# Three stage boundaries of a fused two-block kernel: next weights fetched and split early, attention's first maxima in two banks, first output tile begun in the merge

## The reference

```python
h = rms_norm(x, norm_gain[l]) * (1 + scale[:, None]) + shift[:, None]
aq, ak, av, ag, bz, bg, nq, nk, nv, ng = jnp.split(h @ w_in[l], SPLIT_POINTS, axis=-1)
```

```python
merged = gate_fox * (y_fox @ w_o_fox[i]) + gate_rwkv * (y_rwkv @ w_o_rwkv[i])
x = x + merged @ w_out[i]
h2 = rmsnorm(x, g_ffn[i])
```

## Time and profile before

| what | value |
|---|---|
| time, median of 3 runs | 3684.66 us (3683.51 to 3690.55) |
| the profiled execution's own time | 3686.16 us |
| its span, first to last instruction | 3684.2 us |
| TensorE (PE) busy | 3479.1 us, 94% |
| VectorE (DVE) busy | 2001.4 us, 54% |
| GpSimd (POOL) busy | 1869.1 us, 51% |
| ScalarE (ACT) busy | 1226.0 us, 33% |
| mean granted TensorE clock | 0.975 |

### The profile page before, as it was taken

The page is one execution under the profiler, slowest core; times in us unless marked ns, Lnnn a source line. Parts: engine busy times, 40 slices in busy tenths (PEclk is TensorE's granted clock), DMA queues, the critical chain, the costliest instruction groups (busy, mean ns, idle before and its releaser), DMA issues. The chain is left out here.

```text
span 3684.2 us, 53898 instructions
## 1 busy us (share of the span) xinstructions
PE 3479.1 (94%) x22186; PEld 2661.5 (72%) x22186; DVE 2001.4 (54%) x2268; ACT 1226.0 (33%) x1751; POOL 1869.1 (51%) x1036
## 2 busy tenths in 40 slices
PE   5999899899899999899999999989999999999999
PEld 5888544568788644578887777876578788878877
DVE  4443567662454477553656734545552888883141
ACT  3225444441223344432223422335411444431020
POOL 1444466543354466533445643314544799964443
PEclk9999999999999899999999999989999999999999
DMA  5112200225111200122221220020043122234202
GB/s 187 39 35 75 57 1 1 79 85 213 58 35 66 54 1 1 50 104 70 98 74 49 81 89 24 4 109 1 11 144 137 58 86 82 79 113 164 88 26 74
DMA packets 102074, 257.94 MB, mean 70 GB/s; under 512 B 29248, under 2 KB 38336, under 8 KB 100944
## 3 DMA queue, kind: packets, MB, share of 16 engines
q1 hardware_dynamic: 90960, 217.39, 17.3%
q10 hardware_dynamic: 10880, 37.23, 2.9%
HBM read 200.02 MB, written 54.56 MB: 69 GB/s over the span
## 5 line engine op out<-in xcount | busy, mean ns | idle before, releaser
L2083 PE MATMUL acc<-h_hi,weights_hi 128*128 128x512 f32 (+1 forms) x928 | 347.4, 374 | 8.2 <-DVE h_lo L2252 5.8
L1173 DVE TENSOR_REDUCE part_max<-aux 128x1 f32<-128x428 f32 (+5 forms) x468 | 253.0, 582 | 161.3 <-PE aux L977 113.7
L2084 PE MATMUL acc<-h_lo,weights_hi 128*128 128x512 f32 (+1 forms) x928 | 339.0, 365 | 0.0
L2085 PE MATMUL acc<-h_hi,weights_lo 128*128 128x512 f32 (+1 forms) x928 | 338.7, 365 | 0.0
L2808 PE MATMUL acc<-h_hi,weights_hi 128*128 128x512 f32 x672 | 271.3, 404 | 0.0
L2266 DVE RECIPROCAL arena<-arena 128x512 f32<-128x512 f32 (+1 forms) x48 | 141.7, 2953 | 223.2 <-ACT arena L2229 223.2
L2810 PE MATMUL acc<-h_hi,weights_lo 128*128 128x512 f32 x672 | 262.9, 391 | 0.0
L2809 PE MATMUL acc<-h_lo,weights_hi 128*128 128x512 f32 x672 | 262.5, 391 | 0.0
L1147 ACT ACTIVATE probs<-acc 128x1024 f32<-128x1024 f32 (+1 forms) x168 | 168.5, 1003 | 262.0 <-PE acc L1016 261.5
L1029 PE MATMUL acc<-probs,v_tok 128*64 128x512 f32 (+3 forms) x864 | 221.6, 593 | 2.5 <-DVE inverse L1195 2.5
L2083 PEld LDWEIGHTS acc<-h_hi,weights_hi 128*128 128x128 f32 x928 | 175.7, 189 | 42.7 <-issue 10.6
(11 more groups left out here) (560 smaller groups left out, 8925.5 us busy)
## 6 DMA issues: line engine op xcount, KB each, us to landing
weights<-in_w_in SPq DMA_DIRECT2D x44, 512.0 KB, 3.4
arena<-in_w_mod SPq DMA_DIRECT2D x6, 2048.0 KB, 9.9
weights<-in_w_up SPq DMA_DIRECT2D x24, 512.0 KB, 4.3
weights<-in_w_out SPq DMA_DIRECT2D x22, 512.0 KB, 4.7
weight_sums<-feed_forward_spill SPq DMA_DIRECT2D x22, 512.0 KB, 4.6
xT<-in_w_up SPq DMA_DIRECT2D x20, 512.0 KB, 4.3
mixer_gates<-arena SPq DMA_DIRECT2D x32, 256.0 KB, 2.1
weights<-in_w_gates SPq DMA_DIRECT2D x16, 512.0 KB, 3.8
```

The lines of the kernel that those rows point to most:

```text
L1173: nc.vector.tensor_reduce(part_max[:, b % 2, j, hh, i:i + 1], max_tile(m)[:, hh, 0:cw], AX_X, ALU.max, negate=True).then_inc(max_done, 1)
L2083: nc.tensor.matmul(out, w_hi[:, b, k, :], hi[:, k, cols], start=(k == 0), stop=False)
L2084: nc.tensor.matmul(out, w_hi[:, b, k, :], lo[:, k, cols], start=False, stop=False)
L2085: return nc.tensor.matmul(out, w_lo[:, b, k, :], hi[:, k, cols], start=False, stop=(k == KD - 1))
```

## The change

It has three parts. (a) Layer 0's `gemm_residual` also fetches and parts the first two tiles of layer 1's `w_in`, and layer 1's `project` takes them from there; before the means TensorE runs `keep_busy` 10, after them 4. (b) `rwkv_finish` ends with `keep_busy` 24 on TensorE; in the forgetting attention all eight pieces ahead go by turns to the two places, with waits to fit, and the pauses are 2 products each. (c) `gemm_merge` multiplies k-tiles 0 to 6 of output tile 0 into `aux`, and `gemm_residual` only k-tile 7 of it.

```diff
@@ multiply
     for b in range(2 if not maker else 0):
...
+        if first_in is not None and b == 0:
+            for c0, cn in chunks:
+                out, cols, k = first_in[:, c0:c0 + cn], slice(c0, c0 + cn), nk - 1
+                nc.tensor.matmul(out, w.hi[:, 0, k, :], rhs[0][:, k, cols], start=False, stop=False)
+                nc.tensor.matmul(out, w.hi[:, 0, k, :], rhs[1][:, k, cols], start=False, stop=False)
+                mm = nc.tensor.matmul(out, w.lo[:, 0, k, :], rhs[0][:, k, cols], start=False, stop=True)
+            mm.then_inc(acc_ready, 1)
             continue
@@ gemm_residual, SP
+                    for b, tile in enumerate(next_first):
+                        sp.wait_ge(w.parted, n + 1 + b)
+                        sp.dma_start(w.raw[:, b], tile).then_inc(w.loaded[b], 16)
@@ gemm_residual, TensorE (mean_by_two is False throughout)
                 if squares and not late:
                     if not beside:
                         keep_busy(pg, pg.aux[:, 1], 10)
-                    pe.wait_ge(sq_added, n - 1)
+                    else:
+                        pe.wait_ge(acc_free, n + 1)
+                        keep_busy(pg, pg.acc[:, 0], 10)
+                        pe.wait_ge(beside.added, n - 2)
+                    pe.wait_ge(sq_added, n - 2 if mean_by_two else n - 1)
...
                     mm.then_inc(mean_ready, 1)
                     if beside:
+                        keep_busy(pg, pg.acc[:, 0], 4)
@@ gemm_residual, GpSimd
                 part_weights(nc, pool, w, acc_ready, n)
+                for b in range(len(next_first)):
+                    pool.wait_ge(w.loaded[b], 16 * (n // 2 + 1))
+                    pool.wait_ge(acc_ready, n + 1 + b)
+                    nc.gpsimd.tensor_tensor(w.hi[:, b], w.raw[:, b], w.ones, ALU.mult).then_inc(next_rounded, 1)
+                    pool.wait_ge(next_rounded, b + 1)
+                    nc.gpsimd.tensor_tensor(w.lo[:, b], w.raw[:, b], full(w.hi[:, b]), ALU.subtract).then_inc(next_parted, 1)
@@ gemm_residual, VectorE
+                        done = first_in if first_in is not None and t == 0 else pg.acc[:, t % 2]
@@ pair_attention
+        m_ahead = [j for kind, j, *_ in order[:n_ahead] if kind == "max"] if own_keys else []
-            return score_slots[1].rearrange(...) if pieces[m][0] == 0 and m % 2 else pg.aux
+            return score_slots[1].rearrange(...) if (pieces[m][0] == 0 or m in m_ahead) and m % 2 else pg.aux
-                        if b >= 1:
+                        if b >= 1 and not (m in m_ahead and m - 1 in m_ahead):
                             pe.wait_ge(max_done, 2 * m - 1 + hh)
                         elif m >= 2:
                             pe.wait_ge(max_done, 2 * m - 3 + hh)
+                    if e == 1 and own_keys:
+                        pe.wait_ge(max_done, 2 * len(m_ahead))
-                            keep_busy(pg, outs[1], first_idle if j == 0 else 2 if pieces[j][0] == 0 else 4)
+                            keep_busy(pg, outs[1], first_idle if j == 0 else 2)
@@ project (layer 1 now as layer 0: SP's two fetches and POOL's two partings are gone)
-    done_before = 2 if opened else 0
+    done_before = 2
-                if not opened:
-                    fetch(0)
-                    fetch(1)
-                    keep_busy(pg, pg.acc[:, 0], 12 if opened else 36)
+                    keep_busy(pg, pg.acc[:, 0], 12)
@@ first_block
+                if l:
+                    weights = ahead.raw, ahead.hi, ahead.lo
+                              next_first=() if last else [I["w_in"][l + 1, t] for t in range(2)])
@@ gemm_merge, TensorE
                 multiply(pg, pe, w, y, pg.acc, MAIN, nk, acc_ready, acc_free, 2 * KD, turns=2, begun=True)
+                pe.wait_ge(ahead.parted, 2)
+                for k in range(KD - 1):
+                    pe.wait_ge(merged_parted, k + 2)
+                    for c, (c0, cw) in enumerate(MAIN):
+                        cols = slice(c0, c0 + cw)
+                        nc.tensor.matmul(pg.aux[:, c], ahead.hi[:, 0, k, :], hi[:, k, cols], start=(k == 0), stop=False)
+                        nc.tensor.matmul(pg.aux[:, c], ahead.hi[:, 0, k, :], lo[:, k, cols], start=False, stop=False)
+                        nc.tensor.matmul(pg.aux[:, c], ahead.lo[:, 0, k, :], hi[:, k, cols], start=False, stop=False)
@@ forgetting_attention: first_idle 4 becomes 2
@@ rwkv_finish, TensorE
+                pe.wait_ge(scaled, R_TILES - 1)
+                keep_busy(pg, pg.acc[:, 0], 24)
@@ second_block: gemm_residual(..., first_in=flat(pg.aux[:]))
```

More of the change, by code:

```diff
@@ L325, in part_weights, with multiply @@
             nc.gpsimd.tensor_tensor(w.lo[:, b], w.raw[:, b], full(w.hi[:, b]), ALU.subtract).then_inc(w.parted, 1)
-def multiply(pg, pe, w, rhs, acc, chunks, nk, acc_ready, acc_free, n, turns=1, maker=None, beside=None, begun=False):
+def multiply(pg, pe, w, rhs, acc, chunks, nk, acc_ready, acc_free, n, turns=1, maker=None, beside=None, begun=False, first_in=None):
     nc = pg.nc
@@ L436, in _, with gemm_residual @@
                                              func or ACT.Copy).then_inc(acc_free, 1)
-def gemm_residual(pg, cn, w_of, n, rhs, x, parts, nk, store=None, squares=None, maker_in=None, beside_in=None, x_source=None, ahead=None, following=None, late=False):
+def gemm_residual(pg, cn, w_of, n, rhs, x, parts, nk, store=None, squares=None, maker_in=None, beside_in=None, x_source=None, ahead=None, following=None, late=False, next_first=(), first_in=None):
     nc = pg.nc
@@ L459, in gemm_residual @@
             total, ring = squares[0], squares[1:]
+        next_rounded, next_parted = pg.sem("next_rounded"), pg.sem("next_parted")
+        mean_by_two = False
         with nc.Block() as block:
@@ L486, in _ @@
             def _(pe):
-                multiply(pg, pe, w, rhs, pg.acc, chunks, nk, acc_ready, acc_free, n, maker=maker, beside=beside)
+                multiply(pg, pe, w, rhs, pg.acc, chunks, nk, acc_ready, acc_free, n, maker=maker, beside=beside, first_in=first_in)
                 if squares and not late:
@@ L490, in _ @@
                         keep_busy(pg, pg.aux[:, 1], 10)
-                    pe.wait_ge(sq_added, n - 1)
+                    else:
[3 more added lines that the diff above has]
+                    pe.wait_ge(sq_added, n - 2 if mean_by_two else n - 1)
+                    if mean_by_two:
+                        pe.wait_ge(sq_ready, n)
+                    for t in range(width // P):
+                        cols = slice(t * P, (t + 1) * P)
+                        mm = nc.tensor.matmul(pg.aux[:, 0, t:t + 1], total[:, cols], cn["mean"][:, 0:1], start=True, stop=not mean_by_two)
+                        if mean_by_two:
+                            mm = nc.tensor.matmul(pg.aux[:, 0, t:t + 1], ring[(n - 1) % 2][:, cols], cn["mean"][:, 0:1], start=False, stop=True)
+                    mm.then_inc(mean_ready, 1)
                     if beside:
-                        pe.wait_ge(beside.added, n - 2)
-                    for t in range(width // P):
-                        mm = nc.tensor.matmul(pg.aux[:, 0, t:t + 1], total[:, t * P:(t + 1) * P], cn["mean"][:, 0:1], start=True, stop=True)
-                    mm.then_inc(mean_ready, 1)
+                        keep_busy(pg, pg.acc[:, 0], 4)
             @block.gpsimd
@@ L530, in _ @@
                         tile = x[:, t, c0:c0 + cn]
-                        up = nc.vector.scalar_tensor_tensor(tile, pg.acc[:, t % 2, c0:c0 + cn], 1.0 if scale is None else scale(t), tile,
+                        done = first_in if first_in is not None and t == 0 else pg.acc[:, t % 2]
+                        up = nc.vector.scalar_tensor_tensor(tile, done[:, c0:c0 + cn], 1.0 if scale is None else scale(t), tile,
                                                             ALU.mult, ALU.add)
@@ L543, in _ @@
                 elif squares:
-                    add_squares(n - 1)
+                    if not mean_by_two:
+                        add_squares(n - 1)
                     if beside:
@@ L931, in pair_attention @@
         wide = blocks[0][4]
+        m_ahead = [j for kind, j, *_ in order[:n_ahead] if kind == "max"] if own_keys else []
         def max_tile(m):
-            return score_slots[1].rearrange("p (h n) -> p h n", h=2) if pieces[m][0] == 0 and m % 2 else pg.aux
+            return score_slots[1].rearrange("p (h n) -> p h n", h=2) if (pieces[m][0] == 0 or m in m_ahead) and m % 2 else pg.aux
         def score_tile(e):
@@ L2113, in _ @@
             def _(pool):
-                if opened:
-                    pool.sem_inc(parted, 2)
+                pool.sem_inc(parted, 2)
                 for kind, i in order:
@@ L2399, in first_block @@
                 gemm_residual(pg, cn, weight_tiles(I["w_out"][l]), KD, h, x, parts, KD, store=x_dram, squares=squares, maker_in=maker_in,
-                              beside_in=None if last else next_in, ahead=ahead, following=following, late=last)
```

(4 more changed lines are left out.)

5 lines of the change are left out of this document (4 added, 1 removed).

## The result

| | before | after |
|---|---|---|
| median of 5 runs each | 3684.66 us | 3665.84 us (3662.15 to 3667.02) |
| after / before | | 0.9939, 95% interval 0.9928 to 0.9951 |
| span of the profiled execution | 3684.2 us | 3663.9 us |
| mean granted TensorE clock | 0.975 | 0.977 |

The change takes 18.8 us off the median; 3662 was forecast. Lines of the code have moved: products of the projection are L2118 to L2120 (before L2083 to L2085), scalings L2272, sums L551, means L513, spreading L2177, POOL's parting L528 and L530, maxima L1010 and L1016, first scores L1050, DVE's addition L562.

What follows compares the result with a forecast made beforehand. At three stage boundaries TensorE was taken to wait for other engines, then run at half clock. Parts a -5.8, b -7.8 and c -8.6 sum to -22.2 us: 3684.66 becomes 3662.5, predicted as 3662, range 3655 to 3672.

Steps and rivals of the forecast that it cites:

- scalings: Layer 1's start: DVE's first four scalings of x take 3.36 us without POOL beside them, not 9.29; -5.9 us.
- last sum: Layer 0's end: the last sum of squares must share with POOL's `lo` and ends later; +2.1 us.
- means: Before layer 1: the 20 mean records take 0.16 us each after `keep_busy` 10, not 4.21 in all; -1.0 us.
- The four idle products: Behind the means: 8 records of 0.122 us beside ACT's root and DVE's reciprocal; +0.4 us allowed.
- The spreading: Layer 1's start: 20 records at full clock take 3.2 us, not 4.61; -1.4 us.
- the rival: Clock not carried over the boundaries in a and b: a -3.4, b -1.5, c -8.6, total 3671 us; chance 0.16.
- idle products behind the gate: Normalization's end: 48 idle records take 5.9 us, so TensorE ends after DVE; +0.7 us.
- the first pause and pieces 0 to 3: Attention's opening: first pause -1.5 us, pieces 0 to 3 with three pauses -4.9 us, at full clock.
- the row: Attention's opening: 4.4 us before piece 4 becomes 3.8, piece 4 waiting for the queries' rest; -0.6 us.
- pieces 4 to 7: Attention, piece 4 to first scores: three pauses lose two products each, 12 records of 0.122 us; -1.5 us.
- a stage begun earlier ends earlier by as much: Between boundaries: each stage is a chain fed from outside only by DMAs, so savings carry through in full.
- The rival "given back": Behind an earlier start, notably in attention with POOL and ACT: half of a and b lost, -15.4, 3669 us; chance 0.07.

Runs made afterwards that it cites:

- -8.8 alone: The kernel before with only the 42 products of the output projection's first tile in the merge's tail: 3677.01 us, ratio 0.9973.
- a's own median: The kernel before with only layer 1's two weight tiles fetched and parted ahead: 3681.59 us, ratio 0.9984.
- `lo` later: The changed kernel with POOL's second `lo` behind the last sum and 5 idle products in place of 10: 3662.16 us, ratio 0.9932.
- both joined kernels: The changed kernel with `lo` later, no four idle products, 13 at the turns: 3669.95 us; with six more idle products in layer 1's modulation: 3662.72 us.

## Why the prediction was right, and which sizes were off

**Part a: -5.8 forecast, -4.2 and -5.1 measured.** The mechanism held: scalings -6.0 (-5.9 forecast), last sum +2.0 (+2.1), means -1.2 (-1.0). The means' figure is part luck: their products start every 0.11 us at full clock and every 0.21 at half, so twenty take 2.38 and 4.21 us; the 0.16 a product that the forecast took from the earlier trace rows is a mixture of both, and the means after (3.04) happened to be one too, since the clock fell in the middle of them. Two terms failed. The four idle products were put at +0.4 by a record of 0.122 us; they ran at half clock, 0.26 a record (2.06/8), and cost 1.1, as the run without them shows. The spreading was put at -1.4 on the ground that `keep_busy` 10 keeps the clock: it fell all the same at about 942, and the spreading gained nothing in one profile and 0.8 in the other. So at this boundary the rival was right that the clock isn't carried over; it had put a at -3.4. The sum ended at 940.20, 1.35 us behind `lo` (938.85), which is its own length alone (1.49) within 0.14; with `lo` moved behind it, the 2.0 us are gone. The Trainium skill's rule in "SBUF — State Buffer", "SBUF: two separate sides", that VectorE with two SBUF inputs and GpSimd hold the common ports one after the other, would put the end at 940.34. The trace agrees within that 0.14. The prediction had priced that rule at 2.5 us; from its own stamps (`lo` until 938.9, then 1.49) it is 2.2, all but the same as the 2.1 that it took.

**Part b: -7.8 forecast, -8.3 measured.** Term by term, profile after against the earlier trace rows: idle products behind the gate 0.0 (+0.7 forecast, since 48 records took 5.52 us and not 5.9), the first pause and pieces 0 to 3 -5.65 (-6.4), the row -0.5 (-0.6, and TensorE waits for the queries as forecast), pieces 4 to 7 -2.15 (-1.5). The last term was too small because the prediction put the single place's waits at nothing; with the idle products alone they show as 0.6 us. The first pause's and the pieces' work halved less than forecast: its 9.8 us became 5.5 and not 4.9, with no wait in the trace. The choice that carried it, that a short gap (1.1 us here) leaves the clock at full, held at this boundary in all nine profiles that have the 24 idle products; behind 6.46 us the clock fell in all five that don't.

**Part c: -8.6 forecast, -8.9 and -8.8 measured**, -8.8 alone. Tile 0 ends 0.45 us of boundary and six products behind the last of the 42. Transfers came late for DVE (x at 2757.23) and late for nobody else, as forecast; no wait shows at tile 2. The 0.3 us more than forecast are the boundary, 0.45 us where 0.7 was allowed.

**The sum: -22.2 forecast, -18.8 and -18.2 by the medians.** The parts by their own stages make -21.4 and -22.2, or 0.6 less for b's unlucky first profile. The rest was given back in stretches whose code is equal. One place of it can be named: the turns inside the attention, +4.4 and +1.6 us, where the clock falls behind a gap of 1.85 or 1.18 us. This is one of the prediction's own signs of being wrong, a stretch equal in work that lasts longer than before: the step "a stage begun earlier ends earlier by as much" did not hold in full. The forecast held that a gap of 1.84 us leaves the clock at full, from one row. That was one draw: in the profiles with 8 idle products at the turns and part b in whole or in part, the clock fell there in four of seven, and with 13 in none of three. The rival "given back", at 3669 with 0.07, named the attention but put it on POOL and ACT. It gave back 6.8 us; the turns gave back 4.4 and 1.6, by the clock, so its cause was wrong and its size too large.

What stays open: in the four profiles with the old opening the clock never fell at the turns. Whether a sooner start makes the fall likelier, or four draws were lucky, these runs don't settle. The same holds for the middle: its half clock is 51 to 72 us in the four profiles without part a, 55 to 82 in the ten with it, and its length 0.0 to +1.6 without (mean +0.8) and -1.9 to +8.7 with (mean +3.3). So part a may give back some of its 4 to 5 us there; a's own median, 5.6 us below the kernel before, shows nothing of it. Nor is it shown that `lo` later gains in the time of the whole kernel.

## What to carry to other kernels

Price a stage boundary by stages, not by the median: three parts of 4 to 9 us each came back within 1.2 us in every profile that has them unchanged, where 28 runs of one kernel spread over 15 us. Idle products pay where they fill the time up to an engine that ends the stage anyway (4.6 us for 24 of them), and cost as soon as they end later than it (1.1 us for four at half clock), so count them at the slow clock. When work of GpSimd is moved, look at what DVE does with two SBUF operands beside its new place, and let a semaphore put the two one behind the other. That a stage begun earlier ends earlier by as much holds only while the clock falls at the same places behind it.

## What the runs showed of the hardware

- A gap of TensorE is no safe measure of whether the clock stays: at the first turn, behind 1.85 us, it fell in four profiles of seven; at the third, behind 1.18 us, in two of the seven, one of them the changed kernel's first and not its second; at the middle one, behind 1.15 us, in none. The earlier trace rows show 1.84 without a fall; behind 6.46 it fell in all five.
- DVE's sums of two SBUF operands and POOL's `lo` took turns: `lo` came 1.1 us late for the first sum (3.48 for 2.35), and the second sum 2.0 us late for `lo` (3.45 for 1.49). Each end fits a start behind the other within 0.15 us.
- Twenty one-column products took 4.21 us at half clock (before), 2.38 at full (`lo` later, and both joined kernels), and 3.04 and 2.97 where the clock fell in the middle of them (after, and without the four): 0.21 and 0.11 us from start to start.
- One kernel's time varies from 3679.74 to 3694.54 us in 28 runs, with mean clocks of 0.972 to 0.978.
